# FFN up projection of a two-layer encoder: contraction blocks as the outer loop, token units as the inner one

## Chip, cores and metric

One Trainium2 chip, one of its cores. The metric is the device time of one execution in microseconds, as the median of several runs.

## What is computed

The reference is one inference step of a trunk of two layers for 1024 prompt frames and 32 sample frames (1056 token columns together), width 1024. Each layer is a recurrent mixer (gated DeltaNet, then mLSTM), followed by a SwiGLU FFN, each behind an RMS norm and with a residual add. Only the FFN matters here:

```python
D_MODEL = 1024
FFN_HIDDEN = ((-(-8 * D_MODEL // 3)) + 255) // 256 * 256     # 2816

def swiglu(h, w_gu, w_down):
    gu = h @ w_gu                                            # 1024 -> 2 * 2816
    return (jax.nn.silu(gu[..., :FFN_HIDDEN]) * gu[..., FFN_HIDDEN:]) @ w_down

# in each of the two layers
x = x + y                                                    # y: the mixer
x = x + swiglu(rmsnorm(x, norm_ffn[i]), ffn_w_gu[i], ffn_w_down[i])
```

All of it is in float32.

## The kernel before

Activations lie with channels on the partitions: `x` is [128, 8, 1056], 8 channel blocks of 128 (`KB` = 8) by 1056 token columns. The columns are cut into `NU` = 3 units of 352. A float32 product is made of three float32r matmuls, with both factors split into a high and a low part: high x high (L89), high weights x low activations (L90), low weights x high activations (L91), all into the same PSUM bank. That is `split_product`.

The weights are streamed in blocks of 128 x 1024 by `WeightStream`: SP loads a block into one of two stages, GpSimd splits it in two halves into `hi` (L143) and `lo` (L145), four instructions for a block, into a ring of 6 slots. A slot is split anew when TensorE has finished the block that lay there (`unit_done`).

`ffn_phase` runs once for each layer. It begins with the norm (`Norm`): TensorE sums squares of the three units (L184), ScalarE makes the root and the high part `act_hi`, VectorE scales and makes the low part `act_lo` (L235), three of the eight blocks of it by GpSimd (L257). It has two buffers for three units, so unit 2 comes last, after the others are done. Then come `TURN` = 11 turns. A turn makes two of the 22 hidden blocks and adds what they give to `x`:

- Blocks 0 to 3 are up products: 0 and 2 the silu half, 1 and 3 the other half, of two hidden blocks j = 0 and 1. Each is 3 units x 8 contraction blocks x 3 matmuls = 72 matmuls. Blocks 0 and 2 write PSUM banks 0 to 2, blocks 1 and 3 banks 3 to 5, one bank for each unit. In the kernel before, unit is the outer loop and the contraction block the inner one: a unit's bank is filled by 24 matmuls in a row, then `unit_done` rises, and the next unit follows.
- ScalarE takes the silu of banks 0 to 2 (L403). VectorE multiplies it with banks 3 to 5 into `hid` (L420), ScalarE casts this to `hid_hi` (L408), VectorE subtracts for `hid_lo` (L423). VectorE does these two for unit 0, then 1, then 2.
- The down product goes by unit, and in a unit by output block m = 0 to 7, with 6 matmuls for each. It uses four banks in turn, `DOWN` = (6, 7, 1, 2). VectorE adds each bank to `x` (L430, semaphore `added`), in program order behind the work on `hid`. The down product of unit n waits for `hi_done` and `lo_done` of that unit, and for the add that frees its bank.

Banks 1 and 2 serve both the down product and block 0 of the next turn. So before units 1 and 2 of block 0 TensorE waits until all adds of the turn before are done; unit 0 (bank 0) does not wait for this. Nor does unit 0 of the first turn wait for the norm of units 1 and 2.

Of the kernel before, what the change touches and what calls it, by code (L numbers as in the profile page):

```python
# [34 lines left out]
KB = D // P  # L35
NU = 3
UNIT = TOK // NU
# [25 lines left out]
def unit_cols(n):  # L63
    return slice(n * UNIT, (n + 1) * UNIT)
# [22 lines left out]
def split_product(pe, out, w_hi, w_lo, rhs_hi, rhs_lo, first, last):  # L87

    pe.matmul(out, w_hi, rhs_hi, start=first, stop=False)  # L89
    pe.matmul(out, w_hi, rhs_lo, start=False, stop=False)  # L90
    return pe.matmul(out, w_lo, rhs_hi, start=False, stop=last)  # L91
# [204 lines left out]
def ffn_phase(nc, tk, gain, w_gu, w_down, tag):  # L296
# [4 lines left out]
    ps, x = tk.ps, tk.x  # L301
    with ExitStack() as ctx:
        sem = semaphores(nc, ctx, tag)
        buf = lambda s, *a: ctx.enter_context(nc.sbuf_tensor(f"{tag}_{s}", *a))
        ws = WeightStream(nc, tk, ctx, sem, tag, B)
# [18 lines left out]
        norm = Norm(nc, tk, sem, buf, gain, slots, silu)  # L324
        unit_done = sem("unit_done")
        silu_done = sem("silu_done")
        hid_done = sem("hid_done")
        hi_done = sem("hid_hi_done")
        lo_done = sem("hid_lo_done")
        added = sem("added")  # L330
# [3 lines left out]
        @block.sync  # L334
        def _(sp):
            norm.sync(sp)
            load(sp, 0)
            with sp.Fori(1, TURN) as t:
                load(sp, t)
# [23 lines left out]
        @block.tensor  # L363
        def _(pe):
            norm.tensor(pe)
            with pe.Fori(0, TURN) as t:
                for b in range(4):
                    ws.wait_ready(pe, t * B + b)
                    for n in range(NU):

                        pe.wait_ge(hid_done if b % 2 else silu_done, t * 6 + (b // 2 * NU + n + 1))
                        if b == 0:
                            norm.wait_split(pe, n)
                        if b == 0 and n >= 1:

                            pe.wait_ge(added, t * (NU * KB) + 4)
                        out = ps[:, b % 2 * NU + n, 0:UNIT]
                        for k in range(KB):
                            mm = split_product(pe, out, ws.hi[:, b, k], ws.lo[:, b, k],
                                               tk.hi[:, k, unit_cols(n)], tk.lo[:, k, unit_cols(n)],  # L380
                                               k == 0, k == KB - 1)
                        mm.then_inc(unit_done, 1)
                ws.wait_ready(pe, t * B + 5)
                for n in range(NU):
                    pe.wait_ge(hi_done, t * 6 + (NU + n + 1))
                    pe.wait_ge(lo_done, t * 6 + (2 * NU + n + 1))
                    for m in range(KB):
                        pe.wait_ge(added, t * (NU * KB) + (n * KB + m + 1))
                        for j in range(2):
                            mm = split_product(pe, ps[:, DOWN[m % 4], 0:UNIT],  # L390
                                               ws.hi[:, 4 + j, m], ws.lo[:, 4 + j, m],
                                               hid_hi[:, j, n], hid_lo[:, j, n], j == 0, j == 1)
                        mm.then_inc(unit_done, 1)
# [1785 lines left out]
```

## Time and profile before

| | |
|---|---|
| runs, us | 3627.48, 3632.41, 3598.75 (median 3627.48) |
| profiled execution, span | 3630.7 us |
| TensorE busy | 3321.0 us (91%) |
| weight loads busy | 3138.1 us |
| VectorE, ScalarE, GpSimd busy | 1368.2, 850.4, 1217.1 us |
| the two FFN phases, from their first up product on | 758.1 us and 758.2 us |
| HBM | 37 GB/s over the span |

Times in rows are us from the start of the span, or durations. PE is TensorE's matmuls, PEld its weight loads, DVE VectorE, ACT ScalarE, POOL GpSimd. Matmuls are pipelined: a matmul's row begins before the one ahead of it has ended, so two starts, not a duration, tell the pace. In a row of the timeline the square brackets give how long the engine was idle before, and what released it. "x4" at the end of a row means that four instructions are drawn together.

### The profile page before, as it was taken

The page shows a single profiled execution, that of the slowest core. Times are in us where ns is not written, and L with a number is a line of the kernel's source. Part 1 is how long each engine was busy: PE and PEld are TensorE (multiplying, and loading weights), DVE is VectorE, ACT ScalarE, POOL GpSimd, SP SyncE. Part 2 cuts the span into 40 slices and gives each one's busy share as a digit, 9 for nine tenths or more (in the row PEclk, how much of TensorE's full clock was granted, in tenths as well). Part 3 has the DMA queues.
Part 4 walks back from the last instruction along what each step waited for, and adds up shares of the span by engine and source line. Part 5 has one row for each costly group of instructions (what it writes and reads, how often), then busy time and mean ns, then how long its engine had stood idle before and what let it go on. Part 6 is the DMA issues. An engine that isn't in the chain of part 4 may idle for free. (4 is left out here: it accounts for less than half of the span.)

```text
span 3630.7 us, 56675 instructions
## 1 busy us (share of the span) xinstructions
PE 3321.0 (91%) x20770; PEld 3138.1 (86%) x20770; DVE 1368.2 (38%) x2586; ACT 850.4 (23%) x1773; POOL 1217.1 (34%) x1044
## 2 busy tenths in 40 slices
PE   6989889888986899999999799999968899999998
PEld 5889889888876789999999688888747899999997
DVE  4555555455543232232232433333322422322323
ACT  2342343344232111101101223333321111011012
POOL 3324233233313454434433231211124544344340
PEclk8999999999998999999999899999869999999999
DMA  3000100100002111111111210100021111111111
GB/s 122 24 21 12 27 18 10 27 21 20 7 3 79 41 49 50 46 40 52 46 40 35 65 26 19 36 18 19 13 78 41 47 52 46 40 52 46 40 35 48
DMA packets 200992, 137.28 MB, mean 38 GB/s; under 512 B 32056, under 2 KB 192624, under 8 KB 200368
## 3 DMA queue, kind: packets, MB, share of 16 engines
q1 hardware_dynamic: 200880, 135.63, 12.8%
q8 instruction: 90, 1.47, 0.2%
q14 instruction: 22, 0.18, 0.0%
HBM read 120.98 MB, written 14.63 MB: 37 GB/s over the span
## 5 line engine op out<-in xcount | busy, mean ns | idle before, releaser
L89 PE MATMUL ps<-act_hi,ffn_hi 128*128 128x352 f32 x2112 | 681.9, 323 | 3.5 <-DVE act_lo L235 3.5
L90 PE MATMUL ps<-act_lo,ffn_hi 128*128 128x352 f32 x2112 | 677.0, 321 | 0.0
L91 PE MATMUL ps<-act_hi,ffn_lo 128*128 128x352 f32 x2112 | 676.4, 320 | 0.0
L143 POOL TENSOR_TENSOR ffn_hi<-ffn_stage,one 128x512 fp32r<-128x512 f32 x264 | 291.2, 1103 | 814.1 <-PE ps L91 766.0
L89 PEld LDWEIGHTS ps<-act_hi,ffn_hi 128*128 128x128 f32 x2112 | 396.2, 188 | 4.2 <-ACT ffn_silu L403 4.0
L90 PEld LDWEIGHTS ps<-act_lo,ffn_hi 128*128 128x128 f32 x2112 | 396.8, 188 | 0.2
L91 PEld LDWEIGHTS ps<-act_hi,ffn_lo 128*128 128x128 f32 x2112 | 395.8, 187 | 0.0
L860 POOL TENSOR_TENSOR gdn_mt_level<-gdn_mt,joins 128x384 f32<-128x384 f32 x168 | 178.5, 1067 | 637.1 <-DVE gdn_qd L1300 357.0
L420 DVE TENSOR_TENSOR ffn_hid<-ffn_silu,ps 128x352 f32<-128x352 f32 x132 | 68.8, 522 | 783.7 <-PE ps L91 783.7
L145 POOL TENSOR_TENSOR ffn_lo<-ffn_stage,ffn_hi 128x512 fp32r<-128x512 f32 x264 | 342.1, 1296 | 20.7
L89 PE MATMUL ps<-ffn_hid_hi,ffn_hi 128*128 128x352 f32 x1056 | 340.6, 323 | 0.0
L430 DVE TENSOR_TENSOR x<-x,ps 128x352 f32<-128x352 f32 x528 | 269.5, 520 | 187.1 <-PE ps L91 187.1
L90 PE MATMUL ps<-ffn_hid_lo,ffn_hi 128*128 128x352 f32 x1056 | 338.3, 320 | 0.0
L91 PE MATMUL ps<-ffn_hid_hi,ffn_lo 128*128 128x352 f32 x1056 | 338.0, 320 | 0.0
L89 PE MATMUL ps<-act_hi,gdn_hi 128*128 128x352 f32 x792 | 293.7, 371 | 21.3 <-POOL gdn_lo L1435 21.3
L90 PE MATMUL ps<-act_lo,gdn_hi 128*128 128x352 f32 x792 | 257.6, 325 | 0.0
L91 PE MATMUL ps<-act_hi,gdn_lo 128*128 128x352 f32 x792 | 257.3, 325 | 0.0
L89 PE MATMUL ps<-act_hi,ml_hi 128*128 128x352 f32 x600 | 208.6, 348 | 22.2 <-POOL ml_lo L2024 21.3
L90 PEld LDWEIGHTS ps<-ffn_hid_lo,ffn_hi 128*128 128x128 f32 x1056 | 198.3, 188 | 0.0
L89 PEld LDWEIGHTS ps<-ffn_hid_hi,ffn_hi 128*128 128x128 f32 x1056 | 198.0, 188 | 0.0
L91 PEld LDWEIGHTS ps<-ffn_hid_hi,ffn_lo 128*128 128x128 f32 x1056 | 197.9, 187 | 0.0
L91 PE MATMUL ps<-act_hi,ml_lo 128*128 128x352 f32 x600 | 193.7, 323 | 0.0
(312 smaller groups left out, 5907.1 us busy)
## 6 DMA issues: line engine op xcount, KB each, us to landing
ffn_stage<-in_ffn_w_gu SPq DMA_DIRECT2D x88, 512.0 KB, 3.9
ffn_stage<-in_ffn_w_down SPq DMA_DIRECT2D x44, 512.0 KB, 3.5
gdn_stage<-in_gdn_w_in SPq DMA_DIRECT2D x32, 512.0 KB, 4.4
x_kept<-x SPq DMA_DIRECT2D x2, 4224.0 KB, 12.8
x<-x_kept SPq DMA_DIRECT2D x2, 4224.0 KB, 13.4
ml_stage<-in_ml_w_in SPq DMA_DIRECT2D x16, 512.0 KB, 4.5
load_rows<-in_x_prompt SPq DMA_DIRECT2D x8, 512.0 KB, 4.5
gdn_out_stage<-in_gdn_w_out SPq DMA_DIRECT2D x8, 512.0 KB, 4.3
```

The source lines that it names most:

```text
L89: pe.matmul(out, w_hi, rhs_hi, start=first, stop=False)
L90: pe.matmul(out, w_hi, rhs_lo, start=False, stop=False)
L91: return pe.matmul(out, w_lo, rhs_hi, start=False, stop=last)
L143: nc.gpsimd.tensor_tensor(hi, st, one, ALU.mult).then_inc(self.hi_done, 1)
L145: op = nc.gpsimd.tensor_tensor(lo, st, hi.bitcast(F32), ALU.subtract)
L420: nc.vector.tensor_tensor(hid[:, n], silu[:, n], ps[:, NU + n, 0:UNIT], ALU.mult).then_inc(hid_done, 1)
L430: nc.vector.tensor_tensor(x[:, m, unit_cols(n)], x[:, m, unit_cols(n)], ps[:, DOWN[m % 4], 0:UNIT], ALU.add).then_inc(added, 1)
L860: nc.gpsimd.tensor_tensor(mt_l[:, i % 2], mt[:], tk.joins[:, l][:, None, :].to_broadcast([P, BATCHES, P]), ALU.mult).then_inc(level_masked, 1)
```

## The change

Only the up products in `ffn_phase` change. For each of the blocks 0 to 3, the contraction block k becomes the outer loop. Within it, the high x high matmul is issued for units 0, 1, 2, then high x low for the three, then low x high for the three; each unit keeps its own bank, so that three accumulations are open at once and the output bank changes with every matmul. `unit_done` rises three times, with the last three matmuls of a block. The waits of the units are drawn together ahead of a block: TensorE waits there until the silu (or hidden) work on all three units is done, and in block 0 also for the norm of all three units and for all adds of the turn before. The down product and the other engines' programs are as they were.

```diff
             with pe.Fori(0, TURN) as t:
                 for b in range(4):
                     ws.wait_ready(pe, t * B + b)
-                    for n in range(NU):
-
-                        pe.wait_ge(hid_done if b % 2 else silu_done, t * 6 + (b // 2 * NU + n + 1))
-                        if b == 0:
-                            norm.wait_split(pe, n)
-                        if b == 0 and n >= 1:
-
-                            pe.wait_ge(added, t * (NU * KB) + 4)
-                        out = ps[:, b % 2 * NU + n, 0:UNIT]
-                        for k in range(KB):
-                            mm = split_product(pe, out, ws.hi[:, b, k], ws.lo[:, b, k],
-                                               tk.hi[:, k, unit_cols(n)], tk.lo[:, k, unit_cols(n)],
-                                               k == 0, k == KB - 1)
-                        mm.then_inc(unit_done, 1)
+                    pe.wait_ge(hid_done if b % 2 else silu_done, t * 6 + (b // 2 * NU + NU))
+                    if b == 0:
+                        norm.wait_split(pe, NU - 1)
+                        pe.wait_ge(added, t * (NU * KB) + 4)
+                    out = lambda n: ps[:, b % 2 * NU + n, 0:UNIT]
+                    for k in range(KB):
+                        for n in range(NU):
+                            pe.matmul(out(n), ws.hi[:, b, k], tk.hi[:, k, unit_cols(n)], start=k == 0, stop=False)
+                        for n in range(NU):
+                            pe.matmul(out(n), ws.hi[:, b, k], tk.lo[:, k, unit_cols(n)], start=False, stop=False)
+                        for n in range(NU):
+                            mm = pe.matmul(out(n), ws.lo[:, b, k], tk.hi[:, k, unit_cols(n)], start=False,
+                                           stop=k == KB - 1)
+                            if k == KB - 1:
+                                mm.then_inc(unit_done, 1)
```

## Rows read from the trace of the kernel before

**Rows 1.** The page, its first line.

```profile
span 3630.7 us, 56675 instructions
```

**Rows 2.** Busy by stretch: length, PE, PEld, DVE, ACT, POOL, granted clock, DMA share, GB/s.

```profile
1283.00:2041.10 758.10, 756.29 (x4754) 755.58 (x4752) 232.29 (x405) 80.64 (x147) 300.95 (x253) 1.00 0.14 42
```

**Rows 3.** The page's costliest groups: busy us, mean ns of one, idle before.

```profile
L89 PE MATMUL ps<-act_hi,ffn_hi 128*128 128x352 f32 x2112 | 681.9, 323 | 3.5 <-DVE act_lo L235 3.5
...
L90 PEld LDWEIGHTS ps<-act_lo,ffn_hi 128*128 128x128 f32 x2112 | 396.8, 188 | 0.2
```

**Rows 4.** Timeline (start, length) of TensorE at the end of block 3.

```profile
1399.78 0.32 PE L91 MATMUL ps<-act_hi,ffn_lo 128*128 128x352 f32 x1
1399.94 0.32 PE L89 MATMUL ps<-ffn_hid_hi,ffn_hi 128*128 128x352 f32 x1
```

**Rows 5.** Timeline of VectorE in the same turn.

```profile
1400.29 0.52 DVE L420 TENSOR_TENSOR ffn_hid<-ffn_silu,ps 128x352 f32<-128x352 f32 x1 [2.21 <-PE ps L91]
1401.37 1.60 DVE L423 TENSOR_TENSOR ffn_hid_lo<-ffn_hid,ffn_hid_hi 128x352 fp32r<-128x352 f32 x1 [0.55 <-ACT ffn_hid_hi L408]
1402.89 1.80 DVE L430 TENSOR_TENSOR x<-x,ps 128x352 f32<-128x352 f32 x4
1404.90 0.52 DVE L430 TENSOR_TENSOR x<-x,ps 128x352 f32<-128x352 f32 x1 [0.21 <-PE ps L91]
...
1423.02 0.52 DVE L430 TENSOR_TENSOR x<-x,ps 128x352 f32<-128x352 f32 x1 [0.43 <-PE ps L91]
```

**Rows 6.** Timeline of ScalarE: the cast of unit 2, and two turns' first instruction.

```profile
1358.23 1.28 ACT L403 ACT_TABLE_LOAD   x1 [25.57 <-PE ps L91]
...
1400.85 0.49 ACT L408 CAST ffn_hid_hi<-ffn_hid 128x352 fp32r<-128x352 f32 x1 [3.33 <-DVE ffn_hid L420]
...
1426.90 1.28 ACT L403 ACT_TABLE_LOAD   x1 [25.57 <-PE ps L91]
```

**Rows 7.** Timeline of GpSimd at the end of block 3.

```profile
1400.18 1.04 POOL L143 TENSOR_TENSOR ffn_hi<-ffn_stage,one 128x512 fp32r<-128x512 f32 x1 [6.58 <-PE ps L91]
1401.30 1.28 POOL L145 TENSOR_TENSOR ffn_lo<-ffn_stage,ffn_hi 128x512 fp32r<-128x512 f32 x1
1402.54 1.32 POOL L143 TENSOR_TENSOR ffn_hi<-ffn_stage,one 128x512 fp32r<-128x512 f32 x1
1403.95 1.29 POOL L145 TENSOR_TENSOR ffn_lo<-ffn_stage,ffn_hi 128x512 fp32r<-128x512 f32 x1
```

**Rows 8.** Timeline of GpSimd and VectorE in the first turn.

```profile
1302.24 1.04 POOL L143 TENSOR_TENSOR ffn_hi<-ffn_stage,one 128x512 fp32r<-128x512 f32 x1
1302.28 1.39 DVE L423 TENSOR_TENSOR ffn_hid_lo<-ffn_hid,ffn_hid_hi 128x352 fp32r<-128x352 f32 x1 [0.63 <-ACT ffn_hid_hi L408]
...
1303.36 1.45 POOL L145 TENSOR_TENSOR ffn_lo<-ffn_stage,ffn_hi 128x512 fp32r<-128x512 f32 x1
```

**Rows 9.** Timeline at the start of the first FFN phase.

```profile
1283.08 0.59 PE L89 MATMUL ps<-act_hi,ffn_hi 128*128 128x352 f32 x1
...
1290.17 2.74 DVE L235 TENSOR_TENSOR act_lo<-ffn_slot,act_hi 128x1760 fp32r<-128x1760 f32 x1 [1.45 <-ACT act_hi L214]
...
1293.02 0.40 PE L89 MATMUL ps<-act_hi,ffn_hi 128*128 128x352 f32 x1 [1.76 <-DVE act_lo L235]
```

**Rows 10.** Timeline of TensorE after a long idle stretch, in the output projection.

```profile
1148.83 0.66 PE L89 MATMUL ps<-act_hi,gdn_out_hi 128*128 128x352 f32 x1 [20.31 <-POOL gdn_out_lo L145]
1149.29 0.50 PE L90 MATMUL ps<-act_lo,gdn_out_hi 128*128 128x352 f32 x1
...
1153.69 0.39 PE L90 MATMUL ps<-act_lo,gdn_out_hi 128*128 128x352 f32 x1
```

**Rows 11.** Busy by stretch, in the DeltaNet phase and in the output projection.

```profile
1151.00:1153.80 2.80, 2.80 (x11) 2.80 (x11) 0.00 (x0) 0.00 (x0) 2.39 (x3) 0.50 1.01 434
...
341.40:345.00 3.60, 1.52 (x11) 1.52 (x12) 3.56 (x7) 0.81 (x3) 3.22 (x4) 0.98 0.00 0
345.00:348.00 3.00, 3.00 (x15) 3.00 (x14) 0.52 (x2) 1.35 (x3) 0.94 (x1) 0.50 0.00 0
```

## The prediction

> **What bounds the kernel now.** I read the table of busy times by stretch first. The two FFN phases are 758.1 and 758.2 us of a span of 3630.7 us, and in such a phase TensorE is busy for 756.3 us at full granted clock [rows 1, 2]. So nothing waits there that TensorE could use: its pace is the bound. A turn lasts 1426.90 - 1358.23 = 68.67 us [rows 6] and holds 432 matmuls (288 up, 144 down), so 68.67 / 432 = 0.159 us each, from start to start. The row's 0.32 us is twice that, because neighbours overlap. VectorE, ScalarE and GpSimd have slack; their work counts only where TensorE has to wait for one particular piece of it. I then read the three places where this can happen: the end of block 3, the end of a turn, the start of the phase.
>
> **What the change leaves alone.** The number of matmuls (3 x 2112 up over both phases) and of weight loads stays: the kernel before already issues one load per matmul, also where the second product has the same weights as the first (2112 loads on L90) [rows 3]. So no load is saved, unless something drops repeated ones, and nothing does today.
>
> Would alternating banks or equal weights make a matmul cheaper? Three readings say no. The down products change bank after 6 matmuls: 19 adds lie between 1404.90 and 1423.02, so 18.12 / 19 / 6 = 0.159 us per matmul [rows 5]. The whole turn, two thirds of which changes bank only after 24, has the same 0.159. And L90, whose weights equal those of L89 before it, starts no sooner. I take 0.
>
> **What it adds.** Sums are in the time of the profiled execution; its span is 3.2 us above the median of the runs (3630.7 against 3627.5), so the sum goes on top of either.
>
> *1. End of block 3 to the first down product, 22 times.* Now, units 0 and 1 are ready long before the down product of unit 0 starts, at 1399.94, 0.16 us after the last up matmul [rows 4]. Afterwards all three units end together, in the last three matmuls, 0.16 us apart, and the down product of unit 0 waits for a multiply (L420), a cast (L408) and a subtract (L423). The last unit shows this chain today: multiply 1400.29 for 0.52, cast 1400.85 for 0.49, subtract at 1401.37 [rows 5, 6]. Unit 0 will end two matmuls earlier than unit 2, so I shift by 0.32: multiply 1399.97, cast 1400.53, subtract wanted at 1401.05.
>
> Here GpSimd comes in. Its four splits start at 1400.18, released by the same block end, and the subtract took 1.60 instead of 0.53 us: it ended at 1402.97, 0.39 after the split of 1401.30 had ended (2.58) [rows 5, 7]. In another place a subtract that started 0.04 after a split took 1.39 and ended 1303.67, 0.39 after it [rows 8]. So the subtract waits for the running split and gets the turn next. At 1401.05 the split of 1400.18 to 1401.22 runs: the subtract ends at 1401.61. If it met no split it would end 1401.58, if it missed its turn 1402.97.
>
> TensorE restarts 0.11 us after its releaser (1292.91 to 1293.02) and its first matmul is 0.40 long instead of 0.32 [rows 9]. So the down product starts at 1401.72, 1.78 late, with 0.08 more: **1.86 us x 22 = 41 us** (if the turn is missed, 3.22 x 22 = 71).
>
> *2. The fifth down product, 20 times.* VectorE does all three units before it adds, and the down products have four banks. Unit 1: multiply 1401.53, cast 1402.09, subtract wanted 1402.61; the split delayed by unit 0 ends about 1402.75 (1.45 long, as [rows 8] has it), so the subtract ends 1403.14. Unit 2: multiply 1403.06, subtract wanted 1404.14; the fourth split starts about 1404.11, by 0.03 first, and ends 1405.40, the subtract 1405.79. The first add then ends at 1406.23 (it starts 0.08 before the end of the subtract, as at 1402.89) and the fifth product starts at 1406.34. Untroubled it would start at 1401.80 + 24 x 0.159 = 1405.61. That is 0.73 late, with the restart **0.81 us x 20 = 16 us** (the last turn of a phase has no splits). If VectorE is first in that close race, the add ends 1.0 us earlier and this term is 0; I take the larger, since today the splits win at such distances (0.07 us) [rows 5, 7]. Later adds go at 0.45 each (four in 1.80) against 0.95 per product, so nothing more is late.
>
> *3. Turn boundary, 20 times.* Block 0 now starts with unit 0 right behind the 144 down matmuls, at 1399.94 + 144 x 0.159 = 1422.83, while the last add runs from 1423.02 to 1423.54 [rows 4, 5]; the wait for `added` stands only before units 1 and 2. Afterwards it stands before everything: start at 1423.65, 0.83 late, and 0.08: **0.91 x 20 = 18 us**.
>
> *4. Start of a phase, twice.* Now units 0 and 1 of block 0 run from 1283.08, in the shade of the norm of unit 2, and TensorE idles 1.76 us until its low part is subtracted [rows 9]. Afterwards it idles from the end of the sums, about 1283.5, until 1293.02, and the 48 matmuls come then: 48 x 0.159 = 7.6 us. After 9.5 us of idleness I expect the lower clock. After an idle stretch of 20.31 us the granted clock was 0.50 (1.2 GHz) and the matmuls came 0.293 apart (15 steps from 1149.29 to 1153.69) [rows 10, 11]. The 16 steps from 1148.83 took 4.86 us where 16 x 0.159 = 2.5 would do, so 2.3 us were lost; I take 2.2. **2 x 9.8 = 20 us** (15 without the clock).
>
> *Costed at nothing.* Block 2 waits for the silus of all units (a table load of 1.28 us, then three of about 0.5, some 3 us) and block 3 for three hidden chains (about 5.7 us by part 2). Both lie beside a block of 72 x 0.159 = 11.4 us. Behind the waits of blocks 1 to 3 TensorE alone is queued. Releases for the weight splits come at a block's end as before, and so do the weight transfers behind them on SP's queue.
>
> Sum: 41 + 16 + 18 + 20 = **95 us**, 3627.5 + 95 = **3722 us** (3726 in a profile).
>
> **Rivals.**
>
> *A. The stalls cost more.* The subtract misses its turn (+30), or the clock falls in the new gaps. Against it: the gap of 1.76 us is as long as the new one and the granted clock stays 1.00 [rows 2, 9]. For it: in sparser work, with 1.52 us busy in 3.60, the clock was 0.50 in the next 3 us [rows 11]. Three us at half pace lose 1.4; in all 22 turns +31. Either gives about 3753. Chance 0.17.
>
> *B. Matmuls get cheaper, so that it is not slower by 1%.* At the lower clock a matmul takes 0.293 us, 352 columns at 1.2 GHz [rows 10, 11]; twice that clock would be 0.147, but 0.159 is seen. The 12 ns on top belong to something other than columns. If it is the adding into the bank just written, or loading weights that are already there, the new order could save up to 12.3 ns x 6336 = 78 us: 3644. It decides from (95 - 36) / 6336 = 9.3 ns on. Against it stand the three readings above. The Trainium skill ("TensorE: Matmul & The Clock Gate", section "Back-to-back issue gap") gives columns / 2.4 + 2.5 ns for a warm matmul by itself, 149 ns here; the trace does not agree, and by it the change would give back 62 us (3660), if the order were what holds the pace up. Chance 0.11.
>
> *C. Faster by over 1%.* Even with all 78 us back, terms 1 to 4 would have to fall to 42 us, less than half. Nothing in the rows says so. Chance 0.04.
>
> **Numbers.** Forecast 0.68, with an own range of 3700 (term 2 nothing, no low clock) to 3740; A 0.17, B 0.11, C 0.04. The range reaches from 3665 (part of B) to 3765 (A and a little more). This kernel's measurement tells about 1% from no change. Faster by over 1% 0.04, within 1% 0.11, slower by over 1% 0.85.
>
> **What would show it.** Steps 1 and 3: idle of TensorE of about 1.6 us before L89's successor on the hidden units, released by `ffn_hid_lo`, and about 0.7 us before block 0, released by the add into `x`; turns of 68.7 + 3.6 = 72.3 us. Step 2: a third gap, 3.9 us after the first. Step 4: no up matmul before about 1293, then some at the lower clock. No saving: pitch of the up matmuls still 0.159. It goes wrong if that pitch moves (each ns is 6.3 us), or if the subtract of unit 0 meets GpSimd in another phase.

## The result, and the profile after

| | before | after |
|---|---|---|
| median of 4 runs, us | 3623.7 (3598.75 to 3632.41) | 3723.06 (3706.79 to 3745.81) |
| ratio | 1 | 1.0304, 95% interval 1.0263 to 1.0345 |
| profiled execution, span | 3630.7 | 3743.9 |
| first FFN phase, end of the norm's sums to last down product | 757.5 | 810.1 |
| second FFN phase, the same | 757.5 | 808.7 |
| a turn (10 of 11 in a phase) | 68.67 | 72.30, or 73.0 to 73.2 (6 turns) |
| pitch of the up matmuls, ns | 159.0 | 161.9 |

The changed kernel is 3% slower. The medians differ by 99 us; the ratio in the table, 1.0304, is 110 us, and its interval 95 to 125 us. Between the two profiled executions the FFN phases account for 103.8 us of 113.2; 9.3 of the rest lie ahead of the first phase, in code that is the same in both. Such drifts belong to the single execution: 15 runs of the kernel before on another chip took 3591.7 to 3629.5 us. The lengths of the phases and turns are therefore the better measure below, and a time of a single run a rough one.

The number of matmuls and weight loads is the old one. In the page of the changed kernel (busy us, mean ns of one, idle before) the up products now stand under three lines of `ffn_phase`; the busy sums are smaller than in [rows 3] only because three overlapping matmuls of one line are now counted together:

```profile
L376 PE MATMUL ps<-act_hi,ffn_hi 128*128 128x352 f32 x2112 | 461.2, 327 | 31.6 <-DVE act_lo L235 19.4
...
L378 PEld LDWEIGHTS ps<-act_lo,ffn_hi 128*128 128x128 f32 x2112 | 360.2, 189 | 0.0
```

TensorE's waits (who waited for what: us in total, times, longest), where the kernel before has 3.5 us in its FFN phases, twice at the start:

```profile
PE ps L89 <- DVE ffn_hid_lo L424: 35.8, 22, 1.6
...
PE ps L376 <- DVE act_lo L235: 19.4, 2, 9.7
PE ps L376 <- DVE x L431: 12.3, 20, 0.6
PE ps L89 <- DVE x L431: 3.0, 7, 0.5
```

These are the four places of the prediction, with 22, 2 and 20 stalls as counted there, and the fourth (the fifth down product) in fewer turns than forecast. What does not stand here is a cost without any wait: the pitch. Block 1 of a turn starts at 1389.64 and block 3 at 1412.95, 144 matmuls later, 23.31 us or 161.9 ns each; in the kernel before it was 1365.60 to 1388.49, 22.89 us or 159.0 ns. The timeline of TensorE in the changed kernel, and then in the one before:

```profile
1389.64 0.65 PE L376 MATMUL ps<-act_hi,ffn_hi 128*128 128x352 f32 x3
...
1412.95 0.65 PE L376 MATMUL ps<-act_hi,ffn_hi 128*128 128x352 f32 x3
```

```profile
1365.60 0.32 PE L89 MATMUL ps<-act_hi,ffn_hi 128*128 128x352 f32 x1
...
1388.49 0.32 PE L89 MATMUL ps<-act_hi,ffn_hi 128*128 128x352 f32 x1
```

**The end of block 3**, timeline of all engines but the loads in the changed kernel, to be held against [rows 4 to 7]:

```profile
1424.12 0.65 PE L380 MATMUL ps<-act_hi,ffn_lo 128*128 128x352 f32 x3
...
1424.85 1.04 POOL L143 TENSOR_TENSOR ffn_hi<-ffn_stage,one 128x512 fp32r<-128x512 f32 x1 [6.81 <-PE ps L380]
...
1425.19 0.48 ACT L409 CAST ffn_hid_hi<-ffn_hid 128x352 fp32r<-128x352 f32 x1 [11.19 <-DVE ffn_hid L421]
1425.71 0.56 DVE L424 TENSOR_TENSOR ffn_hid_lo<-ffn_hid,ffn_hid_hi 128x352 fp32r<-128x352 f32 x1 [0.55 <-ACT ffn_hid_hi L409]
1425.97 1.45 POOL L145 TENSOR_TENSOR ffn_lo<-ffn_stage,ffn_hi 128x512 fp32r<-128x512 f32 x1
...
1426.40 0.42 PE L89 MATMUL ps<-ffn_hid_hi,ffn_hi 128*128 128x352 f32 x1 [1.63 <-DVE ffn_hid_lo L424]
...
1427.26 0.54 DVE L424 TENSOR_TENSOR ffn_hid_lo<-ffn_hid,ffn_hid_hi 128x352 fp32r<-128x352 f32 x1 [0.55 <-ACT ffn_hid_hi L409]
...
1428.78 1.68 POOL L145 TENSOR_TENSOR ffn_lo<-ffn_stage,ffn_hi 128x512 fp32r<-128x512 f32 x1
1428.78 0.52 DVE L424 TENSOR_TENSOR ffn_hid_lo<-ffn_hid,ffn_hid_hi 128x352 fp32r<-128x352 f32 x1 [0.55 <-ACT ffn_hid_hi L409]
```

The last three up matmuls end together with the block. The subtract of unit 0 starts at 1425.71, while GpSimd's first split runs; it ends at 1426.27 and TensorE starts 0.13 later. In this turn the subtract of unit 2 and the fourth split start in the same hundredth of a microsecond, and VectorE wins: 0.52 against 1.68 us. Nothing is late afterwards. In another turn GpSimd wins (timeline of VectorE and GpSimd, then the start that follows on TensorE):

```profile
1862.58 1.67 DVE L424 TENSOR_TENSOR ffn_hid_lo<-ffn_hid,ffn_hid_hi 128x352 fp32r<-128x352 f32 x1 [0.55 <-ACT ffn_hid_hi L409]
...
1862.58 1.29 POOL L145 TENSOR_TENSOR ffn_lo<-ffn_stage,ffn_hi 128x512 fp32r<-128x512 f32 x1
...
1864.73 0.43 PE L89 MATMUL ps<-ffn_hid_hi,ffn_hi 128*128 128x352 f32 x1 [0.44 <-DVE x L431]
```

Now the subtract takes 1.67 us, the adds begin late, and the fifth down product waits: this is term 2 of the prediction. In all 20 turns with splits the record of the split begins first, by 4 to 9 ns; VectorE wins in 13 turns, where the split leads by 4 or 5 ns, and GpSimd in 7, where it leads by 6 to 9.

### The profile page after: what moved, and what is told of

Its sections match the earlier page's. It is cut to its first block and busy times, and to the rows that moved or that the text cites. A ratio compares the mean times of both kernels' runs of the same rounds, so it can differ in the third digit from the quotient of the medians.

```text
span 3743.9 us, 56565 instructions
## 1 busy us (share of the span) xinstructions
PE 3366.9 (90%) x20770; PEld 3169.7 (85%) x20770; DVE 1329.5 (36%) x2586; ACT 839.7 (22%) x1773; POOL 1236.6 (33%) x1044
## 5 line engine op out<-in xcount | busy, mean ns | idle before, releaser
L376 PE MATMUL ps<-act_hi,ffn_hi 128*128 128x352 f32 x2112 | 461.2, 327 | 31.6 <-DVE act_lo L235 19.4
L380 PE MATMUL ps<-act_hi,ffn_lo 128*128 128x352 f32 x2112 | 456.8, 324 | 0.0
L378 PE MATMUL ps<-act_lo,ffn_hi 128*128 128x352 f32 x2112 | 456.6, 325 | 0.0
L376 PEld LDWEIGHTS ps<-act_hi,ffn_hi 128*128 128x128 f32 x2112 | 360.5, 190 | 38.5 <-issue 20.5
L89 PE MATMUL ps<-ffn_hid_hi,ffn_hi 128*128 128x352 f32 x1056 | 343.8, 326 | 38.9 <-DVE ffn_hid_lo L424 35.8
L145 POOL TENSOR_TENSOR ffn_lo<-ffn_stage,ffn_hi 128x512 fp32r<-128x512 f32 x264 | 360.4, 1365 | 20.7
L380 PEld LDWEIGHTS ps<-act_hi,ffn_lo 128*128 128x128 f32 x2112 | 364.1, 188 | 0.0
L378 PEld LDWEIGHTS ps<-act_lo,ffn_hi 128*128 128x128 f32 x2112 | 360.2, 189 | 0.0
```

The source lines that it names most:

```text
L145: op = nc.gpsimd.tensor_tensor(lo, st, hi.bitcast(F32), ALU.subtract)
L376: pe.matmul(out(n), ws.hi[:, b, k], tk.hi[:, k, unit_cols(n)], start=k == 0, stop=False)
L378: pe.matmul(out(n), ws.hi[:, b, k], tk.lo[:, k, unit_cols(n)], start=False, stop=False)
L380: mm = pe.matmul(out(n), ws.lo[:, b, k], tk.hi[:, k, unit_cols(n)], start=False, stop=k == KB - 1)
```

## The experiments

The theory after the result: the stalls come from where the waits stand and from units ending together (terms 1 to 4), and the longer pitch is a fifth cost, of the order of the matmuls. The first rival was that pitch and stalls have one cause, the joint waits. The first four runs part these. Of each kernel only the FFN up projection (or what the diff shows) is changed. Pitches are worked out from the starts of blocks, as above.

### The waits without the new order

```diff
-                    out = lambda n: ps[:, b % 2 * NU + n, 0:UNIT]
-                    for k in range(KB): ...      # three units inside
+                    for n in range(NU):
+                        out = ps[:, b % 2 * NU + n, 0:UNIT]
+                        for k in range(KB):
+                            mm = split_product(...)
+                        mm.then_inc(unit_done, 1)
```

> The matmuls of the up products in their old order (unit outermost, each product of three into one bank), but with the waits of the changed kernel: all three units are waited for ahead of a block. Theory (the stalls come from where the waits stand and from units ending together; the longer pitch of 161.9 ns comes from the order of the matmuls): pitch back at 159.0 ns, no gap at the end of block 3, the gap of 0.78 us at the turn boundary and the 10 us at each phase start stay. Turn 68.67 + 0.86 = 69.5 us, time 3624 + 17 + 20 = 3661 us. Rival (the pitch rises because of the waits or of the three banks being freed together): pitch stays 161.9 ns, turn 70.4 us, time 3680 us.

Measured: pitch 159.0 ns, turns 69.57 us, no gap at the end of block 3. Median of 7 runs 3643.1 us against 3612.8 of the kernel before on the same chip: 30 us more, ratio 1.0091 (1.0061 to 1.0120), 22 to 43 us. TensorE's waits:

```profile
PE ps L89 <- DVE act_lo L235: 19.4, 2, 9.7
PE ps L89 <- DVE x L427: 12.3, 20, 0.6
```

They are the same 19.4 and 12.3 us as in the changed kernel. In this profile the two FFN phases are 38.7 us longer than in the kernel before (1553.7 against 1515.0 us), where terms 3 and 4 make 37. So these terms are the joint waits alone, and the pitch is not theirs.

### Block 3 in the old order

```diff
                 for b in range(4):
                     ws.wait_ready(pe, t * B + b)
+                    if b == 3:
+                        ...      # the lines of the kernel before: unit outermost, its own waits
+                        continue
```

> The changed kernel with block 3 alone in the old order. Theory: the down product of unit 0 no longer waits for a multiply, cast and subtract, so both the 1.8 us before it and the later gap before the fifth down product vanish, and a quarter of the longer pitch goes (72 x 2.9 ns = 0.21 us). Turn 72.30 - 1.87 - 0.21 = 70.2 us; phases 22 x 2.1 + 6 = 52 us shorter in all, about 3671 us. Rival (TensorE waits there for the weights' split and not for the hidden part): turn stays at 72.1 us.

Measured: turns 70.20 us, as expected, and FFN phases 52.7 us shorter than in the changed kernel (1566.1 against 1618.8), where 52 were expected. The single run took 3688.2 us, 17 more than expected; that difference lies outside the phases. No wait for `ffn_hid_lo` is left, nor one at the fifth down product. The last up matmuls and the first down product in this kernel's timeline:

```profile
1416.40 0.32 PE L91 MATMUL ps<-act_hi,ffn_lo 128*128 128x352 f32 x1
1416.57 0.32 PE L89 MATMUL ps<-ffn_hid_hi,ffn_hi 128*128 128x352 f32 x1
```

### Blocks 0 and 3 in the old order

The diff is that above with `if b in (0, 3):`.

> The changed kernel with blocks 0 and 3 in the old order, waits included; the new order is left in blocks 1 and 2. Theory: all stalls vanish and only the pitch of 144 matmuls in a turn stays 2.9 ns longer. Turn 68.67 + 0.42 = 69.1 us, time 3624 + 9 = 3633 us, not told from before. Rival (blocks 1 and 2 have hidden costs, their joint waits for silu and hidden work): turn 70 us or more, 3650 us or more.

Measured: turns 69.11 us, and a median of 3618.8 us over 10 runs against 3612.8: ratio 1.0016 (0.9992 to 1.0040). All stalls but the old one at a phase start are gone:

```profile
PE ps L89 <- DVE act_lo L235: 3.6, 2, 1.9
```

With contraction outermost in two of four blocks, the kernel is within noise of the one before; the 9 us (0.25%) expected from the pitch lie inside the interval. The profile shows them: its phases are 9.6 us longer than before (1524.6 us). So the joint waits of blocks 1 and 2 are hidden, as costed.

### GpSimd's splits moved away from VectorE's subtracts

```diff
                     pool.wait_ge(unit_done, t * U + (NU * (b + 1) if b < 4 else U))
+                    if b == 3:
+                        pool.wait_ge(lo_done, t * 6 + NU)
```

> The changed kernel, but GpSimd begins the split into slot 3 only when VectorE has made the three low parts at the end of block 3. Theory (VectorE's subtract waits for a running split of GpSimd): every subtract takes 0.53 us, the gap before the fifth down product is gone in all turns, all 20 turns between take 72.27 us; the gap before the down product itself changes by less than 0.1 us, because a subtract that gets the next turn after a split loses only 0.03 us there. Time about 3717 us. Rival (the extra gap of 8 turns has another cause, as a late bank): it stays, with turns of 73.0 us among them. A second rival: the late split makes block 3 of the next turn wait for its weights; it has 40 us, so this would show as a gap there.

Measured: turns of 72.2 to 72.5 us, 3708.8 us in one run. The fifth product waits in none of them, and the wait before the down product is 35.2 us in 22 where it was 35.8. No gap appears before block 3 of the next turn, as the second rival would have it. The three subtracts of the end of a block 3 in this kernel:

```profile
1395.87 0.53 DVE L426 TENSOR_TENSOR ffn_hid_lo<-ffn_hid,ffn_hid_hi 128x352 fp32r<-128x352 f32 x1 [0.55 <-ACT ffn_hid_hi L411]
...
1397.38 0.53 DVE L426 TENSOR_TENSOR ffn_hid_lo<-ffn_hid,ffn_hid_hi 128x352 fp32r<-128x352 f32 x1 [0.55 <-ACT ffn_hid_hi L411]
...
1398.89 0.53 DVE L426 TENSOR_TENSOR ffn_hid_lo<-ffn_hid,ffn_hid_hi 128x352 fp32r<-128x352 f32 x1 [0.55 <-ACT ffn_hid_hi L411]
```

So term 1 is the chain of three instructions, to which the splits add 0.03 us, and term 2 is the meeting of the two engines.

### What lengthens the pitch: the bank?

The next runs ask for the 2.9 ns. The first theories: B, the bank that changes with every matmul; O, the order of the operands.

`banks_turn`, built on the kernel with the old order and the joint waits (`unit_done` rises by three with the last matmul):

```diff
-                        out = ps[:, b % 2 * NU + n, 0:UNIT]
+                        out = [ps[:, b % 2 * NU + (n + p) % NU, 0:UNIT] for p in range(3)]
                         for k in range(KB):
-                            mm = split_product(pe, out, ...)
+                            # high x high into out[0], high x low into out[1], low x high into out[2]
```

> Up products in the old order of operands (unit outermost, then contraction block, then the three products), but each of a triple's three matmuls goes to another of the block's three banks, so the bank changes with every matmul as in the changed kernel. The three parts of a sum are thus not added up: the hidden values are wrong, the work is the same. Waits stand as in the changed kernel. Theory B (changing the bank with every matmul costs the 2.9 ns): up pitch 161.9 ns. Theory O (the order in which weights and activations are read costs it): up pitch 159.0 ns. All units are released together at the end, so the gap of 1.8 us before the down product should be there (here unit 0 is released with the last matmul: about 0.3 us more, 2.1 us).

`one_bank`, built on the changed kernel:

```diff
+                    last = k == KB - 1
-                    out = lambda n: ps[:, b % 2 * NU + n, 0:UNIT]
+                    out = lambda n: ps[:, b % 2 * NU + (n if last else 0), 0:UNIT]
```

with the start flags to match.

> The order of matmuls and operands of the changed kernel, but for the first seven contraction blocks all three units are added into unit 0's bank, so that the bank does not change; the last contraction block goes to the units' own banks. The sums are wrong, the work is the same. Theory B (the changing bank costs 2.9 ns): up pitch 159.0 ns in the first 63 of 72 matmuls. Theory O (the order of operands): 161.9 ns there. If both orders matter a little, it lies between, and banks_turn tells the other part.

Measured: `banks_turn` 159.0 ns (block 2 at 1394.75, block 3 at 1406.19: 11.44 us for 72), `one_bank` 161.9 ns (1350.23 to 1373.54: 23.31 us for 144). The bank makes no difference at all, in either order; theory B falls. It is the order of the matmuls and their operands, for the waits and the banks are ruled out.

`banks_turn` shows a second thing. Its unit 0 is released with the last matmul, the subtract is wanted after the second split has begun, and misses its turn. The gap is 2.97 us in 20 of 22 turns, instead of 1.63 (63.3 us in all), which is the dear end of term 1 in the prediction (3.22 late); the expectation had missed it. And in 13 of these 20 turns the clock falls behind the gap. TensorE's timeline and two stretches of busy time (length, PE, PEld, DVE, ACT, POOL, granted clock):

```profile
1420.78 0.42 PE L89 MATMUL ps<-ffn_hid_hi,ffn_hi 128*128 128x352 f32 x1 [2.98 <-DVE ffn_hid_lo L421]
...
1421.43 0.49 PE L89 MATMUL ps<-ffn_hid_hi,ffn_hi 128*128 128x352 f32 x1
```

```profile
1345.00:1350.00 5.00, 2.03 (x13) 2.03 (x14) 3.48 (x5) 1.16 (x3) 4.76 (x4) 1.00 0.00 0
...
1421.00:1424.00 3.00, 3.00 (x12) 3.00 (x12) 1.90 (x5) 0.97 (x2) 2.22 (x2) 0.54 0.00 0
```

The turns are 72.8 us long with the full clock (one is 73.1) and 74.4 to 74.6 with the fall. The single run took 3762.8 us. So rival A of the prediction is real, with both its halves, 1.3 us of idleness away.

### Contraction outermost, but triples kept

```diff
                     for k in range(KB):
                         for n in range(NU):
-                            ...      # one product for all units, then the next
+                            mm = split_product(pe, out(n), ws.hi[:, b, k], ws.lo[:, b, k],
+                                               tk.hi[:, k, unit_cols(n)], tk.lo[:, k, unit_cols(n)],
+                                               k == 0, k == KB - 1)
```

> Contraction block outermost and unit inner as in the changed kernel, but the three products of a unit stay together (high x high, high x low, low x high into one bank, then the next unit), so the bank changes with every third matmul and weights alternate as before. Theory B (cost per change of bank): 159.0 + 2.9 / 3 = 159.9 ns, turns about 71.7 us. Theory O: if it is the weights' order 159.0 ns, if it is the activations' order 161.9 ns. Stalls: unit 0 ends 6 matmuls before unit 2 (0.96 us instead of 0.32), so its subtract is wanted 0.64 us sooner, before GpSimd's first split has begun; the gap before the down product falls from 1.8 to about 1.15 us.

Measured: 158.9 ns in some turns and 160.0 in others, 3713.7 us in one run. So contraction outermost by itself lengthens the pitch by 1 ns at most. One and the same order shows two paces here. The stall was misjudged: 20 of 22 gaps before the down product stay at 1.8 us late, since the subtract is then wanted at 1400.41 on the clock of [rows 7], and the split of 1400.18 has begun. It waits for the same split's end. Only in the last turn of a phase, without splits, is the start 1.13 us late. The release of unit 0 can move by 0.6 us and nothing comes of it.

### Repeated weights, or the order of activations?

`pairs`, built on the changed kernel:

```diff
                         for n in range(NU):
                             pe.matmul(out(n), ws.hi[:, b, k], tk.hi[:, k, unit_cols(n)], ...)
-                        for n in range(NU):
                             pe.matmul(out(n), ws.hi[:, b, k], tk.lo[:, k, unit_cols(n)], ...)
```

> The changed kernel with the high x high and high x low products of a unit next to each other (n0 high, n0 low, n1 high, n1 low, n2 high, n2 low, then low x high for the three units): the runs of equal weights are 6 and 3 long as in the changed kernel, only the activations come in another order. Theory W (loading weights that are already in place costs more than new ones): up pitch 161.9 ns. Theory A (the order in which activations are streamed costs it, three high parts of neighbouring units in a row): up pitch 159 to 160 ns. Stalls as in the changed kernel, turns 72.3 us under W, 71.5 us under A.

`no_repeats`, built on the kernel before:

```diff
                         for k in range(KB):
-                            mm = split_product(...)
+                            # high x high
+                        for k in range(KB):
+                            # high weights x low activations
+                        for k in range(KB):
+                            # low weights x high activations
```

> The kernel before (unit outermost, all its waits), but within a unit the contraction blocks run three times, once for each product, so that weights never repeat; sums are complete. Theory W: each repeat costs some 3 ns (gaps into L90, whose weights repeat, are 161 ns, the others 158), so the pitch falls to about 158.0 ns, a turn to 68.4 us. Theory A: the activations of one part come eight in a row; pitch unchanged or longer, up to 162 ns and 69.5 us a turn. Neither: 159.0 ns.

`swap`, built on the kernel before: the second and the third product of a triple exchanged.

> The kernel before with the last two products of each triple exchanged (high x high, low weights x high activations, high weights x low activations): weights never repeat, the activations' high part is streamed twice in a row. Theory W: pitch about 158.0 ns, as without repeats. Theory A (the same or near activations in a row cost): 160 ns or more. Neither: 159.0 ns.

Measured: `pairs` 161.1 ns (3723.9 us in one run), `no_repeats` 161.6 ns (3623.3 us), `swap` 159.0 ns (3620.2 us), the last from 1365.33 to 1388.22 for 144 matmuls. Theory W falls: weights never repeat in `swap` and in `no_repeats`, and the one is as before and the other is 2.6 ns longer. The number that theory A gave for `swap`, 160 or more, did not come either. What the slow orders share is that the streamed columns (contraction block and unit) move with every matmul or nearly so, where the quick ones stay for three.

### Do the streamed columns decide?

`same_columns`, built on the changed kernel: `unit_cols(0)` in place of `unit_cols(n)` in all three products. `turning_columns`, built on the old order with joint waits:

```diff
                         for k in range(KB):
-                            mm = split_product(...)
+                            cols = [unit_cols((n + p) % NU) for p in range(3)]
+                            # product p streams cols[p]; weights and bank as before
```

> The changed kernel, order, weights and banks included, but all nine up matmuls of a contraction block stream the columns of unit 0 (units 1 and 2 get unit 0's sums, so the output is wrong; the work is the same). Theory C (the pitch grows with how often the streamed column range moves: every third matmul in the kernel before 159.0 ns, every matmul in the changed one 161.9 ns): now it moves with every ninth matmul, pitch 159.0 ns or less, some 158 ns. Theory D (it is the grouping of the weights): 161.9 ns stays. Stalls as in the changed kernel.

> The order of weights and banks of the kernel before (with the waits drawn together ahead of a block), but the three products of a triple stream the columns of three different units (the sums mix units and are wrong; the work is the same). Theory C: the column range moves with every matmul, pitch 161.9 ns, turn 69.57 + 288 x 0.0029 = 70.4 us. Theory D (the grouping of the weights, which is the old one here): 159.0 ns, turn 69.57 us.

Measured: `same_columns` 159.4 ns in nearly all blocks (1385.78 to 1397.26, 11.48 us for 72; 162.9 in the first turn of a phase), `turning_columns` 160.2 ns. Time of the single runs 3722.2 and 3640.3 us.

| order of operands | columns move with every | pitch, ns | also seen in the same run |
|---|---|---|---|
| before, `waits_only`, `banks_turn` | 3rd matmul | 159.0 | |
| `swap` | 3rd | 159.0 | 161.0 in one block of the first turn |
| `triples` | 3rd | 158.9 or 160.0 | |
| `same_columns` | 9th | 159.4 | 162.9 in the first turn of a phase |
| `turning_columns` | matmul | 160.2 | |
| `pairs` | 6 times in 9 | 161.1 | |
| `no_repeats` | matmul | 161.6 | 159.4 in the first turn of the second phase |
| changed kernel, `one_bank` | matmul | 161.9 | |

Holding the columns takes back 2.5 of the 2.9 ns in most blocks, and turning them adds 1.2 to the old order. This points to the streamed columns but does not show them as the cause. With equal movement the pitch is 160.2 to 161.9; and the last column has one order at two paces, up to 3.5 ns apart, at full granted clock, which is more than what the orders differ by.

The down product says the same more plainly. No run changes its order, and it too has two paces: 159.0 ns, and 160.8 ns in 3 of the 22 turns of the changed kernel and in 21 of 22 turns of `no_repeats`. Two neighbouring turns of the changed kernel, each with the first matmul of the down product's unit 1 and the last of unit 2, 95 matmuls later (15.27 us, then 15.10):

```profile
1868.70 0.33 PE L89 MATMUL ps<-ffn_hid_hi,ffn_hi 128*128 128x352 f32 x1
...
1883.97 0.32 PE L91 MATMUL ps<-ffn_hid_hi,ffn_lo 128*128 128x352 f32 x1
...
1941.88 0.32 PE L89 MATMUL ps<-ffn_hid_hi,ffn_hi 128*128 128x352 f32 x1
...
1956.98 0.32 PE L91 MATMUL ps<-ffn_hid_hi,ffn_lo 128*128 128x352 f32 x1
```

So the pace of a stretch hangs not only on its own order, but also on something that it takes over from what ran ahead of it. What that is, and how the addresses of streamed columns and loaded weights fall together, was not tried and stays open. Firm is only the difference that the change makes: 161.9 ns in every undisturbed block of the new order (changed kernel, `late_split`, `one_bank`, and the blocks in that order of `units_in_3` and `units_in_0_3`), and 159.0 to 159.3 in those of the old one.

## Why the prediction was right

**The bound.** It was right that the FFN phase is a chain of matmuls at a fixed pitch, and that every wait put into it shows in full: each stall named was found, at its place, with its releaser.

| term | forecast, us | measured in the profiled execution |
|---|---|---|
| 1, before the down product | 41 (22 x 1.86) | 22 x (1.63 idle + 0.16 overlap lost + 0.1 restart) = 42 |
| 2, fifth down product | 16 (20 x 0.81) | 7 turns by 0.7, and 0.2 more in three of them, whose down product ran at 160.8 ns: 6 |
| 3, turn boundary | 18 (20 x 0.91) | 20 x (0.61 + 0.16 + 0.1) = 17 |
| 4, phase start | 20 | 103.8 less the other lines: 20; by `waits_only`, 38.7 less term 3: 21 |
| pitch | 0 | 6336 x 2.92 ns = 18.5 |
| sum | 95 | 104 in the FFN phases; medians 99 |

The idle time of a row counts from the end of the last matmul, whose last 0.16 us a next one would have overlapped; that is the middle part of a stall in lines 1 and 3.

**Term 1** held in size and mechanism: the subtract of unit 0 was forecast for 0.95 us after the last matmul's end and came 0.94 after it (1424.77 to 1425.71); it waited for the first split and got the next turn. `units_in_3` removed the term, `late_split` showed that the splits carry almost none of it, and `banks_turn` showed its dear end.

**Term 2** was mis-sized for this execution. The step said that the fourth split starts 0.03 us before the subtract of unit 2 and so wins. It does start first in all 20 turns, but by less than 0.01 us, and it wins in only 7; in the other 13 the subtract takes 0.53 us and the term is nothing. The forecast gave both ends and took the dear one for all turns. That isn't simply wrong: in kernels with the same end of block 3 GpSimd wins in 20 turns of 20 (`one_bank` and `pairs`) and in 18 (`same_columns`), and then the term is at its dear end. Of the changed kernel only one execution has a trace, so how the race falls in its others isn't known. A lead of 0.03 us, worked out from two sums, can't be told from a tie, and both ends belong into the range.

**Terms 3 and 4** held. TensorE idled 9.67 us at the phase start, and the clock was low afterwards, as forecast (busy by stretch in the changed kernel, granted clock third from the end):

```profile
1292.80:1302.40 9.60, 0.00 (x0) 0.00 (x0) 6.75 (x9) 3.78 (x4) 4.93 (x2) 0.76 0.00 0
1302.40:1307.00 4.60, 4.56 (x15) 4.57 (x16) 0.00 (x0) 0.00 (x0) 4.44 (x5) 0.50 0.01 4
...
1315.00:2103.00 788.00, 762.02 (x4692) 754.54 (x4690) 206.16 (x396) 72.09 (x143) 293.06 (x241) 1.00 0.13 39
```

**The pitch** is the step that failed. The prediction gave 0, from three readings: a change of bank, equal weights in a row, and the same pitch in two patterns of banks. All three were right in what they said; `banks_turn` and `one_bank` confirm that the bank is free, and `swap` that repeated weights are. But all patterns of the kernel before keep the three products of a unit together and stream a column range for three matmuls in a row (the down product too moves it with every third). The trace of before could not show what another order costs, and the prediction put no bound above nothing on it. It named the price of being wrong (6.3 us for a ns). That the sum of 95 comes so near is in part luck: the miss of +18 stood against one of -10 in term 2, which with GpSimd winning every turn would not have been there.

**Rivals.** B asked for a pitch 9.3 ns shorter; it moved 2.9 ns the other way. The Trainium skill ("TensorE: Matmul & The Clock Gate", section "Back-to-back issue gap") gives columns / 2.4 + 2.5 ns for a warm matmul by itself, by which an estimate for 352 columns is 149 ns. The traces do not agree for this stream: none of the ten orders came below 158.9 ns. A did not come in the changed kernel, whose gaps of 1.63 us left the granted clock at 1.00 over a phase (from 1315 to 2103 us, behind the start of the first, and likewise in the second), but it did in `banks_turn`.

## What to carry over

Where TensorE is the bound with no gap, a loop nest that lets several outputs finish together moves the whole chain of work behind them onto the path; let them finish one after another at least in the last block before a consumer, and the stall is gone. Contraction outermost saves nothing where every matmul loads its weights anyway, as the number of weight loads in the profile tells beforehand. Draw waits together only where the block ahead hides the slowest of them, and give an order of operands that the trace has never shown a price above nothing in the range: here 2.9 ns a matmul were 18 us.

## What the runs showed of the hardware

- The pitch of 352-column float32r matmuls at full clock went from 159.0 ns in the old order of operands to 161.9 in the new, whether the output bank stayed or changed (159.0 either way in the old order, 161.9 either way in the new); in the old order it was 159.0 with and without weights that repeat. It is no function of the order alone: the down product, the same in all runs, ran at 159.0 or at 160.8 ns, both within one execution. The rule stays open.
- A VectorE subtract with both inputs in SBUF waits for the GpSimd split that is running, then goes next: 0.56, 0.54 and 1.67 us where 0.53 is its own length. When both start within 0.01 us, either can win, in one and the same kernel (13 to 7; in `one_bank` and `pairs` 0 to 20).
- Over the gaps of 1.63 us in dense matmuls the granted clock stayed 1.00; after those of 2.97 us it stayed in 7 turns and fell to half in 13, at a cost of about 1.6 us a turn.
